# Attention output computed with stationary values, two heads in two column halves, and the softmax factors transposed once per head pair

## The reference, cut to what matters

```
logits = jnp.einsum('bqhd,bqkhd->bhqk', qb, k_sel) * dh ** -0.5      # + bias, masked
p = jax.nn.softmax(logits, axis=-1)
return jnp.einsum('bhqk,bqkhd->bqhd', p, v_sel)                      # sparse attention (group A)
...
p = jax.nn.softmax(logits, axis=-1)
return jnp.einsum('bhtm,bmhd->bthd', p, vh).reshape(B, T, MEM_W)     # memory attention (group C)
```

## Time and profile before

| what | us |
|---|---|
| median of 3 runs (lowest 2159.5, highest 2165.27) | 2159.62 |
| the profiled execution | 2161.88 |
| its span, first to last instruction | 2160.1 |
| TensorE busy | 2135.3 (99%) |
| VectorE busy | 1050.1 (49%) |
| ScalarE busy | 758.7 (35%) |
| GpSimd busy | 358.9 (17%) |
| mean granted TensorE clock | 0.997 of full speed |

### The profile page before, as it was taken

One profiled execution on the slowest core, in us unless ns is written; L12 is line 12 of the kernel. 1 busy time (PEld: TensorE's weight loads), 2 busy tenths in 40 slices (PEclk: granted clock), 3 DMA queues, 4 the chain that ended last, 5 costly groups with the idle time before them and its releaser, 6 DMA issues.

```text
span 2160.1 us, 31275 instructions
## 1 busy us (share of the span) xinstructions
PE 2135.3 (99%) x12889; PEld 1728.5 (80%) x12889; DVE 1050.1 (49%) x1433; ACT 758.7 (35%) x1046; POOL 358.9 (17%) x295
## 2 busy tenths in 40 slices
PE   8999999999999999999999999999999999999999
PEld 7888888777777888888888888887777778888887
DVE  5333333688656543333343433337876656434322
ACT  5222222474335422222232222234843454222211
POOL 0111011105013411101111010120141135010000
PEclk9999999999999999999999999999999999999999
DMA  5222223221201232222222222332212102222232
GB/s 194 93 95 94 100 91 115 96 98 42 78 32 40 78 106 94 95 92 105 93 98 97 97 97 90 107 115 99 86 44 79 40 21 98 97 97 97 92 107 73
DMA packets 30642, 192.36 MB, mean 89 GB/s; under 512 B 3216, under 2 KB 5392, under 8 KB 11984
## 3 DMA queue, kind: packets, MB, share of 16 engines
q1 hardware_dynamic: 30160, 189.80, 25.0%
q10 hardware_dynamic: 384, 1.14, 0.1%
HBM read 188.70 MB, written 2.10 MB: 88 GB/s over the span
## 4 chain that ended last, share of the span: by engine, by line
PE 89%; DVE 7%; ACT 2%; issue 1%; DMA 0%; SPq 0%; POOL 0%; DVEq 0%; ACTq 0%
PE psum L898 27%; PE psum L900 26%; PE psum L899 26%; PE psum L1328 2%; PE psum L1029 1%; PE psum L1312 1%; DVE wl L1751 1%; PE psum L1201 1%; PE psum L1198 1%; PE psum L1296 1%; DVE acc L1834 1%; PE psum L1232 1%; DVE XL L1766 1%; DVE gkT L1865 0%; DMA raw<-weights 0%
## 5 line engine op out<-in xcount | busy, mean ns | idle before, releaser
L898 PE MATMUL psum<-XH,wh 128*128 128x512 f32 x1904 | 761.7, 400 | 6.1 <-DVE XL L1711 3.2
L900 PE MATMUL psum<-XH,wl 128*128 128x512 f32 x1904 | 743.6, 391 | 0.0
L899 PE MATMUL psum<-XL,wh 128*128 128x512 f32 x1904 | 743.4, 390 | 0.0
L898 PEld LDWEIGHTS psum<-XH,wh 128*128 128x128 f32 x1904 | 358.6, 188 | 94.2 <-issue 18.0
L900 PEld LDWEIGHTS psum<-XH,wl 128*128 128x128 f32 x1904 | 358.5, 188 | 75.7
L899 PEld LDWEIGHTS psum<-XL,wh 128*128 128x128 f32 x1904 | 358.9, 188 | 74.7 <-issue 4.3
L1759 DVE TENSOR_TENSOR wl<-raw,wh 128x2048 fp32r<-128x2048 f32 x88 | 201.8, 2293 | 159.4 <-ACT wh L1398 159.4
L898 PE MATMUL psum<-HH,wh 128*128 128x512 f32 x704 | 273.9, 389 | 0.0
L899 PE MATMUL psum<-HL,wh 128*128 128x512 f32 x704 | 273.9, 389 | 0.0
L900 PE MATMUL psum<-HH,wl 128*128 128x512 f32 x704 | 273.9, 389 | 0.0
L1393 ACT ACTIVATE wh<-raw 128x2048 fp32r<-128x2048 f32 (+1 forms) x84 | 157.2, 1872 | 302.6 <-PE psum L900 302.5
(11 more groups left out here) (251 smaller groups left out, 1992.1 us busy)
## 6 DMA issues: line engine op xcount, KB each, us to landing
raw<-weights SPq DMA_DIRECT2D x143, 1024.0 KB, 4.8
raw<-weights SPq DMA_DIRECT2D x32, 896.0 KB, 4.4
xT<-xt SPq DMA_DIRECT2D x4, 512.0 KB, 7.3
memT<-memt SPq DMA_DIRECT2D x2, 1024.0 KB, 4.8
out<-xT SPq DMA_DIRECT2D x8, 256.0 KB, 6.2
stripsA<-strip_table SPq DMA_DIRECT2D x2, 768.0 KB, 6.7
raw<-weights SPq DMA_DIRECT2D x2, 512.0 KB, 7.1
stripsB<-strip_table SPq DMA_DIRECT2D x2, 512.0 KB, 7.3
```

What stands on the lines that cost most here:

```text
L898: pe.matmul(out_ap, a_hi, b_hi, start=first, stop=False)
L899: pe.matmul(out_ap, a_hi, b_lo, start=False, stop=False)
L900: return pe.matmul(out_ap, a_lo, b_hi, start=False, stop=last)
```

## The change

The value product swaps its operands. The head's values (128 keys x 64) become stationary, pT (keys x 128 queries) moves, and the output has the head's 64 features in the partitions and 128 queries in the columns. The two heads of a pair write the upper and the lower 64 partitions of the same 128 columns of bank 3, so their stationary operands lie in the two column halves of the array. The output is then already transposed; the transposes of oA at the end of a phase go.

The division by the row sums, which was by partition, has to be by column. For each pair VectorE takes the reciprocal of the two sums, spread over 64 columns each (128x128, `rrec`, three buffers), in slot p+1; TensorE transposes it into columns 384 to 511 of bank 3 in slot p+3, ahead of the logits and the values; ScalarE copies the values out of PSUM into oA in slot p+3; VectorE multiplies oA with the transposed factors in slot p+4. The transpose waits for the product of the pair before (jx_done), since there is one place for the factors. At a phase's end ScalarE and VectorE make XH and XL from oA instead of bank 3. Both heads' pT are now waited for before the first value matmul. The buffers rrec and oA lie where EGr of the delta rule lay.

```diff
@@ tensor: attention(slot)
-                        p = slot - 4
-                        if 0 <= p < N_PAIRS and phase_end(p):
-                            b, ph, done = phase(2 * p)
-                            pe.wait_ge(S["o_ev"], done + 1)
-                            for c in range(3 if ph else 2):
-                                mm = pe.transpose(bank[3][:, c * P:(c + 1) * P], oA[:, c * P:(c + 1) * P],
-                                                  const("ident"))
-                            mm.then_inc(S["o_t"], 1)
...
+                        p = slot - 3
+                        if 0 <= p < N_PAIRS:
+                            b, j = job(2 * p)
+                            pe.wait_ge(S["jr_done"], of("jr_done", p + 1))
+                            if p:
+                                pe.wait_ge(S["jx_done"], of("jx_done", p))
+                            else:
+                                pe.wait_ge(S["os_read"], of("os_read", NB))
+                            pe.transpose(bank[3][:, WA:WA + P], rrec[:, p % 3, :], const("ident"))
...
-                            for e in range(2):
-                                n = 2 * p + e
-                                b, j = job(n)
-                                pe.wait_ge(S["jp_odd" if e else "jp_even"], p + 1)
...
-                                for i in range(nt):
-                                    v = (dvN[:, i, at0:at0 + DH] if j < H_A else mvN[:, i, at0:at0 + DH])
-                                    mm = pe.matmul(bank[3][:, at0:at0 + DH], pT[n % 4][:, i * P:(i + 1) * P], v,
                                                    start=(i == 0), stop=(i == nt - 1))
-                                mm.then_inc(S["jv_done"], 1)
+                            b, j = job(2 * p)
+                            pe.wait_ge(S["jp_even"], p + 1)
+                            pe.wait_ge(S["jp_odd"], p + 1)
+                            nt = b + 1 if j < H_A else 2
+                            vals, at0 = (dvN, DH * j) if j < H_A else (mvN, DH * (j - H_A))
+                            for i in range(nt):
+                                for e, r in enumerate(rows):
+                                    mm = pe.matmul(bank[3][r, at0:at0 + P],
+                                                   vals[:, i, at0 + DH * e:at0 + DH * (e + 1)],
+                                                   pT[(2 * p + e) % 4][:, i * P:(i + 1) * P],
                                                    start=(i == 0), stop=(i == nt - 1))
+                                    if i == nt - 1:
+                                        mm.then_inc(S["jv_done"], 1)
@@ scalar: attention(slot), at the end of the slot
+                        p = slot - 3
+                        if 0 <= p < N_PAIRS:
+                            b, j = job(2 * p)
+                            c = (j if j < H_A else j - H_A) // 2
+                            act.wait_ge(S["jv_done"], 2 * p + 2)
+                            if c == 0 and p:
+                                act.wait_ge(S["o_lo"], phase(2 * p)[2])
+                            act.activation(oA[:, c, :], bank[3][:, c * P:(c + 1) * P], ACT.Copy).then_inc(S["jo_done"], 1)
@@ vector: attention(slot), at the start of the slot
+                        if 0 <= p < N_PAIRS:
+                            b, j = job(2 * p)
+                            c = (j if j < H_A else j - H_A) // 2
+                            dve.wait_ge(S["jo_done"], of("jo_done", p + 1))
+                            dve.tensor_tensor(oA[:, c, :], oA[:, c, :], bank[3][:, WA:WA + P], ALU.mult
+                                              ).then_inc(S["jx_done"], 1)
...
-                            chain.step(dve.reciprocal(rrec[:, b % 2, j0:j0 + nh], rsum[:, b % 2, j0:j0 + nh]))
-                            chain.join()
@@ vector: attention(slot), after the maxima
-                            dve.wait_ge(S["jv_done"], 2 * p + 2)
-                            r = rrec[:, b % 2, j0:j0 + nh].unsqueeze(2).to_broadcast([P, nh, DH])
-                            dve.tensor_tensor(oA[:, 0:nh * DH].rearrange("p (h d) -> p h d", h=nh),
-                                              bank[3][:, 0:nh * DH].rearrange("p (h d) -> p h d", h=nh), r,
-                                              ALU.mult).then_inc(S["o_ev"], 1)
+                        p = slot - 1
+                        if 0 <= p < N_PAIRS:
+                            b, j = job(2 * p)
+                            dve.wait_ge(S["je_done"], 2 * p + 2)
+                            dve.reciprocal(rrec[:, p % 3, :].rearrange("p (e d) -> p e d", e=2),
+                                           rsum[:, b % 2, j:j + 2].unsqueeze(2).to_broadcast([P, 2, DH])
+                                           ).then_inc(S["jr_done"], 1)
```

More of the change, by code:

```diff
@@ L367 @@
                   w_done=4, vp_ps=8, vn_done=8, s_ps=7, s_done=7, sd_done=6, sz_done=1, o_ps=8, oc_done=4,
-                  os_ps=4, os_read=4, or_done=4, op_done=4, og_done=4, gh_done=3, gl_done=3, cb_done=18, tap_done=9, pr_done=24, ex_done=16, hf_hi=3, hf_lo=3,
+                  os_ps=4, os_read=4, or_done=4, op_done=4, jr_done=N_PAIRS, jo_done=N_PAIRS, jx_done=N_PAIRS, og_done=4, gh_done=3, gl_done=3, cb_done=18, tap_done=9, pr_done=24, ex_done=16, hf_hi=3, hf_lo=3,
                   sm_t=1, sp_e=1, sp_b=1, g_ready=1)
@@ L524 @@
 jl_done jm_done je_done jtr_done jp_even jp_odd jv_done
-o_ev o_t o_hi o_lo
+o_hi o_lo
 """.split()
@@ L595, in hybrid_trunk @@
         rsum = sb("rsum", [P, 2, JOBS])
-        rrec = sb("rrec", [P, 2, JOBS])
+        sb("behind_rsum", [P, 2, JOBS])
         memr = sb("memr", [P, 2])
@@ L630, in hybrid_trunk @@
         kg = sb("kg", [P, NB, WB])
+        with ExitStack() as third:
+            rrec = sb("rrec", [P, 3, P], F32, third)
+            oA = sb("oA", [P, 3, P], F32, third)
         EGr = sb("EGr", [P, 3, T])
@@ L649, in hybrid_trunk @@
         stripsC = sb("stripsC", [P, 1, T])
-        oA = sb("oA", [P, WA])
         strips = [(stripsA, stripsB, stripsC)[j // 3 + j // 5][:, (0, 1, 2, 0, 1, 0)[j], :] for j in range(H_A)]
@@ L1637, in attention @@
                             b, ph, done = phase(2 * p)
-                            act.wait_ge(S["o_t"], done + 1)
+                            act.wait_ge(S["jx_done"], of("jx_done", p + 1))
                             c0, c1 = (0, 3) if ph else (6, 8)
                             act.activation(XH[:, c0:c1, b * P:(b + 1) * P],
-                                           bank[3][:, 0:P * (c1 - c0)].rearrange("p (c t) -> p c t", t=P),
-                                           ACT.Copy).then_inc(S["o_hi"], 1)
+                                           oA[:, 0:c1 - c0, :], ACT.Copy).then_inc(S["o_hi"], 1)
                         p = slot - 2
@@ L2008, in attention @@
                             sl = (slice(None), slice(c0, c1), slice(b * P, (b + 1) * P))
[L2009 to L2016, removed]
-                            chain.step(dve.reciprocal(rrec[:, b % 2, j0:j0 + nh], rsum[:, b % 2, j0:j0 + nh]))
-                            chain.join()
+                            dve.tensor_tensor(XL[sl], oA[:, 0:c1 - c0, :], XH[sl].bitcast(F32), ALU.subtract
+                                              ).then_inc(S["o_lo"], 1)
                         p = slot
```

## The result

The changed kernel takes 2178.62 us (median; 2176.92 to 2183.09) against 2159.56 us of the kernel before in the same set: ratio 1.0078, 95% interval 1.0062 to 1.0094. By the medians it is 19.1 us slower, by the ratio 16.8 (13.4 to 20.3). The forecast had the sign and the mechanism, and about double the size: 2194, that is +34.4, with 2182 to 2207 as its own range and 2172 to 2218 as the wide one. 2178.6 lies in the wide range and outside the forecast's own, and the loss is about half of what was foretold, so the sum has to be taken apart.

A forecast was written before the change was run, and what follows sets the result against it. TensorE set the pace before, with VectorE nearly full; after, VectorE would be late in every slot. Per layer +1.3, +15.4, -2.4 and +3 for clock make 17.3, for two 34.6: 2194 us, range 2182 to 2207.

The forecast's parts named there:

- change of shape: On TensorE, between matmuls of different shapes: 0.14 us charged a pair around the values, 0.20 us between transpose and logits.
- clock: In the attention, two more 3.4 us stretches at 1.2 GHz a layer, charged +3 us; bounds 0 and 11.
- the ring: In each attention slot, VectorE's product, TensorE's transpose and logits, then VectorE's maxima wait in turn: 0.95 to 1.45 us idle.
- slots 5 to 19: Fourteen attention slots of a layer: VectorE needs 68.2 us against 52.8, so +15.4 us.
- behind slot 19: Last four pairs of a layer, VectorE light: TensorE gains 2.9 us, less 0.5 for their new chain, so -2.4.
- check on one slot: VectorE's durations and wait added up for one memory-pair slot with selection: 5.25 us, against 4.24 before.
- forced idleness: VectorE waiting for logits in the 14 slots: 16.5 us, or 13.7 after 2.8 us of phase-end work fits in.
- Rival 4: Attention: the clock falls in most slots, costing 11 instead of 3 us a layer: 2210 us; chance 13%.
- (2): Rival on VectorE: the reciprocal runs at the ordinary rate, 0.29 us, giving 2166 us; chance 8%.
- (3): Rival on TensorE's value product: the two column halves take turns instead of running at once: 2201 us; chance 8%.
- (1): Rival: TensorE still sets the attention's pace and the factors come in time: 2144 us; chance 4%.
- (5): Rival: part of the ring is hidden where VectorE runs ahead without selection, half of the sum: about 2177; chance 9%.

The follow-up runs named there:

- the doubled load: The changed kernel with a second, unused 128x128 reciprocal a pair on VectorE, ahead of the real one: 2212.47 us, ratio 1.0241 to the kernel before.
- e10: The changed kernel with a pair's value matmuls issued head after head instead of alternating between the column halves: 2186.34 us, ratio 1.0113 to the kernel before.
- e9: The changed kernel with the factors' step moved behind the logits and the reciprocal taken of the pair's two sums only: 2147.88 us, ratio 0.9941.
- e8: The changed kernel with ScalarE copying values and factors together, the next factor step waiting for that copy, plus e9's small reciprocal and move: 2148.27 us, ratio 0.9938.
- e1: The changed kernel with the reciprocal of the pair's two sums only, spread by two small TensorE matmuls instead of the transpose: 2165.27 us, ratio 1.0022.
- e4: As e8, but a pair's value matmuls go head after head instead of alternating between the column halves: 2154.62 us, ratio 0.9967 to the kernel before.

## Why the prediction was right in kind and wrong in size

**What held.** The reciprocal: 1.01 us by the line through three widths, 0.946 measured. The product: 0.29, 0.271 measured. The wait and what is queued behind it: TensorE's wait for L2016 is the largest of the attention. The gap of VectorE in a slot with two tiles: 1.11 us foretold, 1.10 measured (644.10 to 645.20), though its first part was 0.14 instead of 0.06 us and the change of shape 0.12 instead of 0.20. The rate of the halves: a block of 12 passes takes 0.76 us up to the next matmul (681.11 to 681.87, above) where 12 passes took 12 x 0.114 = 1.37, and the forecast had 0.68 and the change of shape. That change was charged with 0.14 us and takes 0.12 (from the last pass of the values to the next matmul 0.203 us instead of 0.084). That VectorE is late in every slot: the doubled load shows it, and e10's stretch, which is no longer with more work on TensorE.

**What failed.** Per layer, in us, with the clock taken out at 1.6 us for 3.4 us at half clock in slots 0 to 5 (the bound of 1.7 less a little, and 22.11 against 20.56 us for layer 0 and 1 of the kernel before, with 6.8 and 3.4 us at half clock) and at 0.75 in the ring. The changed kernel's one such stretch in slots 0 to 5, in layer 0, is taken at nothing, since they last 20.88 and 20.87 us with it and without:

| term | forecast | layer 0 | layer 1 |
|---|---|---|---|
| slots 0 to 5 | +1.3 | +1.9 | +1.9 |
| slots 5 to 19 | +15.4 | +11.1 | +11.1 |
| behind slot 19 | -2.4 | -3.0 | -3.3 |
| clock | +3.0 | -1.6 | +0.6 |
| sum | +17.3 | +8.4 | +10.3 |

In the one profiled execution 2.3 us come on top, from 6.8 us at half clock in the first half-step, far from the change; together that is the span's 21.0.

The step that failed most is the sum of VectorE's busy time for the 14 slots: 39.7 + 18.2 - 3.4 = 54.5 us forecast, 50.75 measured. In the trace of layer 0 these 3.7 us have three parts. 1.0 us is durations: the 28 new instructions last 17.06 us together instead of 18.2, the 11 that went 3.28 instead of 3.4. 0.9 us is in instructions that the change doesn't touch and that are shorter after it, the three weight residues (3.49 instead of 3.86 us) and the eight MAX8 (5.14 instead of 5.49) above all; why, no run shows. The largest part, 1.8 us, is that I added durations to a busy time. A busy time counts overlaps once, and VectorE's instructions overlap: the reciprocal lasts 0.94 us, but the next instruction starts 0.85 us after it (645.88 and 646.73), the product after the addition 0.60 instead of 0.68. What the overlaps take off the sum of durations grew from 5.4 to 7.2 us. The doubled load agrees: 0.946 us of duration made most slots 0.81 longer. The check on one slot carried the same error: 5.25 forecast, 4.86 measured (644.47 to 649.33). The forced idleness was forecast as 13.7 and measured as 14.7, with 1.5 of it from the low clock: right.

The second is the clock. I charged 3 us a layer on top of the ring; that is 7.0 us too much over the two layers, nearly as much as the 7.4 of the first step. The low stretches did come, two or three in slots 5 to 19, where the kernel before has none. But they cost 0.75 us each and not 1.7: inside the ring TensorE has slack, and only the transpose and the logits are on the path. And the low stretch that the kernel before has at its fourth slot was already paid for; in the changed kernel it is 3.4 us instead of 6.8 in layer 0, absent in layer 1, and costs nothing there. The two were forecast as one sign and had two. Rival 4's 11 us stood for a low stretch in each of the 14 slots at 0.8 us; that price was right, but two or three came.

The third is small: behind slot 19 TensorE's gain came in whole, without the 0.5 us set aside for the new chain.

Of the signs that the prediction named, the reciprocals, the released waits and the low stretches were there. Three sizes were off with the sum: VectorE is 78% busy in the slots instead of over 80, they start 4.7 us apart instead of 4.9, and TensorE's wait for the product is 12.4 us in all, about 1 us in each of twelve, instead of 1.2 to 2.

The rivals: (2) falls with the 946 ns. (3) falls with the passes of the two halves 7 ns apart, one such pair every 0.11 us. (1) is false for the changed kernel; e9 and e8 come near it, 2147.9 measured where the rival had 2144, once the logits no longer stand behind the product. The argument against it, that the ring would fill the slots even with a reciprocal at nothing, was right in the changed kernel's order: e1 is that case, 58.59 us where the argument gave 54.1 and 14 x 0.16 more. (Of the other 2.3 us, 2.0 would be its longer factor step, 14 x 0.14, if every slot paid it; that isn't shown.) (4) had the price of a low stretch right and their number wrong. (5), a part of the ring hidden and half of the whole sum left, 2177, hits the figure by accident: the ring's idleness came in full.

What stays open: why load and ring cost about 1.5 us more together than apart, beyond the clock; with e1's longer factor step taken off it would be up to 3.5, and how much of it is load that hides behind TensorE in e9 isn't separated. Open too is why VectorE's untouched instructions are 0.9 us shorter. Two places for the factors within bank 3, so that the product need not be waited for at all, were not tried: VectorE would then read the bank while TensorE writes it. The Trainium skill (PSUM — Partial Sum Buffer, PSUM bank collisions raise a hardware error) says that this is an error on the chip whatever the columns; no run here shows it.

## What to carry to other kernels

When a change makes TensorE wait for a slower engine, look at what stands behind the wait on TensorE's queue. If that is the work which the slower engine needs next, the two engines take turns there, and each slot costs the slower engine's work plus the other's piece between (here 1.1 us of transpose and logits); in this kernel one transpose moved behind the logits turned +0.8% into -0.2%, and a reciprocal of 2 columns instead of 128 on top of it into -0.6%. For such a sum take start-to-start times of instructions, not durations, and charge a low clock only on the part of TensorE's work that is on the path.

## What the runs showed of the hardware

- A VectorE reciprocal of 128x128 float32 takes 946 ns, and the next instruction starts about 850 ns after it; 4, 6 and 24 elements took 168, 181 and 304 ns. That is 6.2 to 6.8 ns an element, where a product of 128x128 takes 271 ns in all. The Trainium skill's repeat count of 8 (VectorE: DVE Perf Modes, First, the fixed hardware budget), read as 8 steps an element at its 0.96 GHz, would have given an estimated 1.2 us; the row decides.
- A stationary operand can be one column read again and again (step zero): two such float32 matmuls against the identity spread and transpose the factors (e1, e8, e9), 0.37 us up to the logits where one transpose took 0.23. This takes the place of a broadcast by VectorE.
- Matmuls in opposite column halves run at once also when their order of issue is not alternating, but a pass overtook at most three passes of the other half issued before it: in turn, a block of 8 passes lost 0.05 us, one of 12 lost 0.27 and one of 16 lost 0.49.
- A stretch of 3.4 us at 1.2 GHz cost about 1.6 us where TensorE set the pace (slots 5 to 19 of e4: 53.39 us in layer 0 with one, 51.83 in layer 1 without) and 0.7 to 0.8 where VectorE did.
